# A Hymba-style layer on one core: mixer and experts joined into one program per engine, with a new order for the last tiles

## The reference

```python
h = concat([meta, x])                          # 4112 rows
hn = rms_norm(h, mix_norm_g)
q, k, v, B, C, H = split(hn @ w_in)            # 512 | 128 | 128 | 512 | 512 | 512 columns
a = sliding_window_sink_attention(rms_norm(q), rms_norm(k), v, sinks, rel_bias)  # 128-row blocks, own and previous keys
c = B * conv3_causal(C * H)
h = h + concat([rms_norm(a), rms_norm(c)]) @ w_out
hn = rms_norm(h, ffn_norm_g)
# router: the best of 4 groups, then the best 2 of its 8 experts, gate = p(group) * softmax(top 2)
# tokens sorted by expert; each expert works through its tokens in blocks of 128 rows
h = h + gate * ((silu(x @ w_gate[e]) * (x @ w_up[e])) @ w_down[e])
return h[16:]
```

## Time and profile before

| | us |
|---|---|
| median of 3 runs | 2775.46 (2773.0 to 2777.52) |
| profiled execution | 2770.24 |
| its span in the trace | 2768.6 |
| TensorE busy in the span | 2646.2 (96%) |
| VectorE busy | 1721.2 (62%) |
| ScalarE busy | 1394.0 (50%) |
| GpSimd busy | 832.8 (30%) |
| transfers, all queues | 495.22 MB, mean 179 GB/s |

### The profile page before, as it was taken

The page is one execution under the profiler, slowest core; times in us unless marked ns, Lnnn a source line. Parts: engine busy times, 40 slices in busy tenths (PEclk is TensorE's granted clock), DMA queues, the critical chain, the costliest instruction groups (busy, mean ns, idle before and its releaser), DMA issues.

```text
span 2768.6 us, 49889 instructions
## 1 busy us (share of the span) xinstructions
PE 2646.2 (96%) x14252; PEld 1820.5 (66%) x14253; DVE 1721.2 (62%) x3920; ACT 1394.0 (50%) x3046; POOL 832.8 (30%) x825
## 2 busy tenths in 40 slices
PE   4999999999999999996599999999999999999997
PEld 2445555555555555553488888888888888888886
DVE  5677777777777777776445456545545444546643
ACT  7665555556555556653234455445545443445533
POOL 1133333233333323331223333223323322333332
PEclk9899999999999999998799999999999999999999
DMA  8376666666666666656556677676767665667763
GB/s 310 85 164 165 155 159 159 151 156 163 165 154 158 159 152 156 165 133 153 183 159 189 197 223 241 191 223 200 240 189 235 204 187 155 180 188 232 241 182 53
DMA packets 546395, 495.22 MB, mean 179 GB/s; under 512 B 411787, under 2 KB 411948, under 8 KB 545340
## 3 DMA queue, kind: packets, MB, share of 16 engines
q1 hardware_dynamic: 517516, 406.08, 52.1%
q0 software_dynamic: 28848, 88.77, 13.7%
HBM read 309.74 MB, written 87.88 MB: 144 GB/s over the span
## 4 chain that ended last, share of the span: by engine, by line
PE 49%; DMA 1%; issue 0%; DVE 0%; POOL 0%; ACT 0%; POOLq 0%; DVEq 0%; ACTq 0%
PE psB L1637 15%; PE psA L1637 15%; PE psF L1637 8%; PE psG L1637 8%; PE psC L1645 1%; PE psD L1645 1%; PE psE L1652 1%; DMA xg<-hn_rows,slots 1%; DMA slots<-slot_table 0%; DMA out_rows<-y,rows_of_y 0%; DVE down_lo L1773 0%; DVE y L1780 0%; POOL out_rows L1573 0%; ACT gT_hi L1757 0%; POOL slots_old L1578 0%
## 5 line engine op out<-in xcount | busy, mean ns | idle before, releaser
L543 PE MATMUL psG<-wi_all,both_xT 128*128 128x512 f16 x1536 | 345.2, 381 | 11.2 <-DMA both_xT<-x 11.2
L543 PEld LDWEIGHTS psG<-wi_all,both_xT 128*128 128x128 f16 x1536 | 148.7, 98 | 188.4 <-DMA both_xT<-x 11.4
L1561 POOL DMA_INDIRECT xg<-hn_rows,slots x80 | 100.8, 1261 | 542.4 <-DMA slots<-slot_table 392.0
L1637 PE MATMUL psB<-up_hi,gT_hi 128*128 128x512 f32 x632 | 254.1, 402 | 0.0
L1637 PE MATMUL psA<-gate_hi,gT_hi 128*128 128x512 f32 x632 | 246.8, 391 | 3.1 <-ACT gT_hi L1757 1.7
L1773 DVE TENSOR_TENSOR down_lo<-wi_all,down_hi 128x512 fp32r<-128x512 f32 x256 | 157.0, 685 | 147.3 <-ACT down_hi L1731 147.3
L1637 PE MATMUL psB<-up_hi,gT_lo 128*128 128x512 f32 x632 | 247.4, 391 | 0.0
L1637 PE MATMUL psA<-gate_hi,gT_lo 128*128 128x512 f32 x632 | 246.9, 391 | 0.0
L1637 PE MATMUL psA<-gate_lo,gT_hi 128*128 128x512 f32 x632 | 246.6, 390 | 0.0
L1637 PE MATMUL psB<-up_lo,gT_hi 128*128 128x512 f32 x632 | 246.3, 390 | 0.0
L1757 ACT ACTIVATE gT_hi<-psC 128x512 fp32r<-128x512 f32 x80 | 47.8, 598 | 384.2 <-PE psC L1645 384.2
(11 more groups left out here) (315 smaller groups left out, 5902.9 us busy)
## 6 DMA issues: line engine op xcount, KB each, us to landing
wi_all<-in_w_gate SPq DMA_DIRECT2D x32, 2048.0 KB, 9.8
wi_all<-in_w_up SPq DMA_DIRECT2D x32, 2048.0 KB, 12.8
wi_all<-in_w_down SPq DMA_DIRECT2D x32, 2048.0 KB, 12.0
xt<-in_x SPq DMA_DIRECT2D x32, 512.0 KB, 3.8
um<-u_rows SPq DMA_DIRECT2D x64, 256.0 KB, 2.8
out_rows<-h SPq DMA_DIRECT2D x32, 512.0 KB, 3.2
xres<-in_x SPq DMA_DIRECT2D x31, 512.0 KB, 4.7
hn_rows<-xres SPq DMA_DIRECT2D x31, 512.0 KB, 2.9
```

Of the source, the lines that this page charges most:

```text
L543: m = nc.tensor.matmul(ps, left[:, l, k, :], weights.half(r, k, n, width), start=(k == opens and j == 0), stop=(k == closes and j == 2))
L1561: pool.indirect_dma_start(xg[:], None, hn_dram, bass.IndirectOffsetOnAxis(ap=slots[:, 0, 0:1], axis=0), bounds_check=SEQ + P - 1).then_inc ...
L1637: m = nc.tensor.matmul(ps[:, :], l[:, k, :], r[:, r_k[n], :], start=(n == 0 and j == 0), stop=(n == len(l_k) - 1 and j == 2))
```

## The change

- `mixer` and `experts` no longer open a block. Each returns one function per engine, and one block runs, on each engine, the mixer's and then the experts' function.
- In place of the barrier, each engine calls `mixed`: six waits on constants, for the last counts, the last router exponentials, the 18 last steps, the last scatter into the lists, and the last stores of output rows and of `hn`. ScalarE's table load and VectorE's clearing of `slots` come before `mixed`, its clearing of `y` after it.
- For that, the semaphores of both stages live to the end, and `slots`, `slots_old`, `rows_of_y` are allocated ahead of the mixer's tiles.
- The last tile's list entries have tiles of their own (`slot_last`, `entry_last`), so that its `place_tokens` doesn't wait for the scatter of the tile before.
- On GpSimd, in every tile, the convolution's first product is put ahead of the wait for `um`, and two semaphore increments are added.
- In the written-out end: on SP `store_u(32)` goes ahead of `turn_a(31)`, `load_shifted(32)` ahead of `load_residual(31)`; on TensorE `values(32)` ahead of `counts_of(30)`, and `out_half(32)` is completed before `route(31)`; on VectorE `place_tokens(29)` goes ahead of `lower_prob(31)`, `attended(32)` ahead of `lower_c(32)`, and `place_tokens(30)` behind `lower_hn(31)`.

```diff
         with ExitStack() as ctx:
-            mixer(nc, ctx, locals())
+            mix, mixed = mixer(nc, ctx, locals())
         with ExitStack() as ctx:
-            experts(nc, ctx, locals())
+            serve = experts(nc, ctx, locals())
+        with nc.Block() as block:
...
+            @block.gpsimd
+            def _(pool):
+                mix["gpsimd"](pool)
+                serve["gpsimd"](pool)
...
+    slot_last, entry_last = sb("slot_last", [P, 2], I32), sb("entry_last", [P, 2, 2], I32)
+
+    def lists(t):
+
+        return (slot_last, entry_last) if isinstance(t, int) and t == TILES else (slot, entry)
...
         turn_hn(t - 2)
+        store_u(t)
         turn_a(t - 1)
-        store_u(t)
+        load_shifted(t)
         load_residual(t - 1)
-        load_shifted(t)
...
         out_half(t - 1, aT_in, FIRST_CHUNKS)
+        values(t)
         counts_of(t - 2, t)
-        values(t)
         out_half(t, cT_in, LAST_CHUNKS)
+        out_half(t, aT_in, FIRST_CHUNKS)
         route(t - 1, t)
-        out_half(t, aT_in, FIRST_CHUNKS)
...
-                after(pool, um_in, t)
                 after(pool, u_s, t)
                 after(pool, c_hi, t - 1)
                 after(pool, c_lo, t - 1)
+                hold(pool, held)
                 g.tensor_tensor(yc[:], u[:], w_cv[:, 2, :], ALU.mult).then_inc(cv.sem, 1)
+                after(pool, um_in, t)
+                hold(pool, held)
                 g.tensor_tensor(um[:, 0, :], um[:, 0, :], w_cv[:, 1, :], ALU.mult).then_inc(cv.sem, 1)
...
-            after(dve, listed, t - 1)
+            where, what = lists(t)
+            gates = what[:].bitcast(F32)
+            if what is entry:
+                after(dve, listed, t - 1)
...
         top_scores(t - 1)
+        place_tokens(t - 3)
         lower_prob(t - 1)
-        place_tokens(t - 3)
...
         choose_experts(t - 2)
+        add_residual(t - 1)
+        attended(t, t - 3)
         lower_c(t)
-        add_residual(t - 1)
-        place_tokens(t - 2)
-        attended(t, t - 3)
         scale_hn(t - 1)
         lower_a(t)
         lower_hn(t - 1)
+        place_tokens(t - 2)
...
+    def mixed(eng):
+
+        eng.wait_ge(cnt_ps.sem, cnt_ps.at(TILES))
+        eng.wait_ge(rt_e.sem, rt_e.at(TILES))
+        eng.wait_ge(last, planned)
+        eng.wait_ge(listed.sem, listed.at(TILES))
+        eng.wait_ge(rows_out.sem, rows_out.at(TILES))
+        eng.wait_ge(hn_out.sem, hn_out.at(TILES))
...
         s.preload_act_table_set("silu_and_others")
+        mixed(act)
...
         v.tensor_copy(slots[:, :, 0], cst[:, C_JUNK:C_JUNK + 1].to_broadcast([P, 4])).then_inc(cleared, 1)
+        mixed(dve)
         v.memset(y[:], 0.0).then_inc(cleared, 1)
```

82 lines of the change are left out of this document (47 added, 35 removed).

## The result

| | before | after |
|---|---|---|
| median | 2774.23 (4 runs, 2769.07 to 2777.52) | 2750.97 (4 runs, 2750.46 to 2751.34) |
| profiled execution | 2770.24 | 2750.93 |
| its span | 2768.6 | 2749.3 |

A forecast was written before the change was run, and what follows sets the result against it. TensorE alone was taken to bound both steady parts, so only the hole between stages could pay: -8.4 to the last list landing and -6.1 at the seam, -14.5 in all, from 2775.46 to 2761.0 us, range 2754 to 2769.5.

The forecast's parts named there:

- The seam: Between mixer and experts: drain and barrier go, saving 6.6 us, less 0.5 for a disturbed gather: -6.1, bounds -6.9 and -4.6.
- the second rival: At the barrier: GpSimd's 6.03 us drain is work someone must await, so the gain there is 0.6; 2767.0, chance 0.10.
- The concern: First gather: SP's next 2 MB load starts earlier, into the gather, costing nothing to 2 us; 0.5 taken.
- project_kv(32): Last tiles: its 2.62 us wait for `place_tokens(29)` goes, so `out_half(31)` ends 2.6 us earlier.
- values(32) to out_half(32): End of mixer: `out_half(32)` starts about 1279.5 and runs its second half at once, before `route(31)`: 7.4 us gained by its end.
- The last list entry and its landing: Tile 32's list scatter: issued 10.3 us earlier, landing about 1320.0 beside the expert load: -8.4, bounds -10.3 and -5.5.
- lower bound of 17.2: Whole kernel: the largest gain from the known bounds, -17.2 against the forecast -14.5, giving a median of 2758.3.
- An edit can only pay, or cost, in the hole: Whole kernel: only about 1273 to 1349 us can change, since TensorE alone sets the time in both stages' steady parts.
- The step to the median: From profile to median: the profiled execution lies 5.2 below the runs' median, so 2755.7 becomes 2761.0.
- The first (the order gives little): End of mixer: `out_half(32)` stays as late as before, leaving only the list wait and barrier gains, -7.1; 2768.4, chance 0.13.
- The third (slower through GpSimd beside VectorE): Steady tiles: GpSimd's earlier product slows VectorE beyond its slack of 1.9 us a tile; 2790 at 2.9 lost, chance 0.05.
- The fourth (more than forecast): Hole: full clock in `out_half(32)`, scatter landing in 2.1, undisturbed gather, earlier start: -19.1, 2756.4, chance 0.10.

The follow-up runs named there:

- no_tokens29: The changed kernel with `place_tokens(29)` behind `lower_prob(31)` again on VectorE: 2755.38 us, 0.9939 of before.
- pe_route_first: The changed kernel with `route(31)` between the two halves of `out_half(32)` again on TensorE: 2751.51 us, 0.9925 of before.
- no_sp: The changed kernel with SP's order of the last tiles as before: 2754.2 us, 0.9938 of before.
- order_gather_safe: The changed kernel with VectorE's old order for tile 32, block counts read later, first `down` loaded after the first gather, second `gate` after the second: 2748.98 us.
- router_early2: The changed kernel with block counts read later, expert loads held behind gathers, and tile 31's router steps earlier: 2747.88 us, 2748.36 us when repeated.
- conv_only: The kernel before with only GpSimd's first convolution product ahead of the wait for `um`: 2769.74 us, 0.9985 of before.
- no_conv: The changed kernel with GpSimd's first convolution product behind the wait for `um` again: 2751.1 us, 0.9924 of before.
- tail_only: The kernel before with only the new written-out orders of the last tiles on SP, TensorE and VectorE: 2762.78 us, 0.9964 of before.
- seam_only: The kernel before with only the joined program, six waits for the barrier and three small tiles allocated earlier: 2768.96 us, 0.9989 of before.
- seam_gather_alone: The kernel before with only the joined program, plus an SP wait holding the second expert's `gate` until the first gather lands: 2766.83 us, 0.9978 of before.
- no_attended_first: The changed kernel with VectorE's order of before for tile 32: 2755.55 us, 0.9947 of before.
- no_dve_pe: The changed kernel with VectorE's order of before for tile 32 and TensorE's end order of before: 2761.67 us, 0.9964 of before.

## Why the prediction was right and wrong

**The seam** (-6.1 forecast). The read of the blocks came 0.35 us after the landing, 0.3 forecast; the drain was a fixed cost of 6.03 us, as assumed, so the second rival falls. The gather was not disturbed and was even faster, 4.7 us instead of 5.3, where I had added 0.5. From landing to product 13.46 us, 14.75 forecast: 1.3 better, nearly all of it from the gather. The concern was right in kind and badly bounded: "nothing to 2 us" for a load that starts into a gather should have been "nothing to 5". That the changed kernel escaped it was luck: it turned on whether the load began 0.1 or 0.7 us before the end of the gather's issue.

**project_kv(32)** (-2.6). The stretch before it is 2.8 shorter. Right, and no_tokens29 gives 2.07 for it with all else changed.

**values(32) to out_half(32).** I gave the start 8.15 us after out_half(31), and it was 7.26: `lower_c(32)` was done 4.7 us after it, as forecast, and the way from there took 2.5 instead of 3.5; the row with the slow first bank (5.04 against 4.44) cost 0.6 of that again. The end came 20.07 after out_half(31), 20.8 forecast. The mechanism for TensorE's order holds: 5.7 us with VectorE's order of before. What the prediction didn't see is that VectorE's new order alone brings 3.7 of it and then costs 1.4. `place_tokens(30)` behind `lower_hn(31)`, taken as costing nothing and given no gain, has 2.2 of the 3.0 us by which `hn` is ready sooner. So the wait of 4.12 us, which the prediction gave to TensorE's order, would have all but gone without it: 0.32 us of it are left in pe_route_first.

**The last list entry and its landing.** From the end of out_half(32) to the second scatter 23.93 us, 23.9 forecast. The landing took 3.98, the 4.0 taken from between the bounds. The Trainium skill's page "DMA: Bandwidth & Descriptors", section "Queues, rings and completion order", has the DMA engines take turns between queues; by that the prediction had a landing near 2.1. The trace lies between: the scatter of tile 32, issued beside the load's last microseconds, took 4.0 us, one of tile 31, well inside it, 6.2. The latter was issued at 1303.91 and the load flowed until about 1315, so it did not stand behind all of it, in which the trace agrees with the page. Of the 2.45 to 2.9 us of wait that the list tile takes away, 0.6 arrive, 1.0 forecast.

**The terms that were missed.** Against the forecast span of 2754.1 the trace has 2749.3, 4.8 less: 2.6 up to `project_kv(32)`, 0.3 to out_half(31), 0.7 in out_half(32), 1.3 in the seam, less 0.15 behind it. The span moved by 19.3, more than the prediction's own lower bound of 17.2. The step that failed is "An edit can only pay, or cost, in the hole": the start was put at nothing, and 2.5 of the 2.6 us lie ahead of the third tile. The windows view there, in before:

```profile
170.00:180.00 10.00, 7.23 (x37) 3.71 (x36) 8.16 (x34) 3.32 (x12) 3.17 (x3) 0.83 0.76 189
```

The same in after:

```profile
170.00:180.00 10.00, 7.71 (x45) 4.11 (x44) 8.46 (x38) 4.26 (x13) 4.39 (x4) 1.00 0.77 211
```

The granted clock was 0.83 and 1.00; 1.3 of the 2.5 us lie behind the wait for VectorE in this stretch, 0.5 in it (2.76 and 2.27 us) and the rest ahead of it. A second such place is from 60 to 120 us, where the clock was 0.86 in both, but 0.77 in no_tokens29, no_sp and order_gather_safe among others. router_early2 shows both cases with one program, so a part of it differs from execution to execution; but all four runs of no_tokens29 took some 2 us more than its wait explains, while seven of the changed kernel's eight lie within 0.9 us, so a part seems to hang on the kernel. Whether it is the joining, or GpSimd's product, which does act in the first tiles, is open: conv_only is 2.9 faster in the median, but no_conv, with the product back behind its wait, is as fast as after.

**The step to the median.** The other 5.2 us were a mistake of method, the step "it lies 5.2 below the median of the runs, so the median becomes". The profiled execution was 5.2 below the median of three, and I carried that distance over as if it belonged to the profiler. In 62 further runs the kernel before took 2767.87 to 2779.31 us with a median of 2772.2, and the time follows the mean granted clock: 2776.0 on average at 0.981 (4 runs), 2772.7 at 0.983 (28), 2768.7 at 0.985 (3). So of the 5.2 the profiled execution was 2.0 on the quick side, and the median of the first three runs 3.2 on the slow side. The changed kernel's four runs in the table have 0.985 to 0.987 and lie within 0.9 us, so its profile equals its median. A forecast made from span to span would have given 2755.7.

**The rivals.** The first (the order gives little) falls: out_half(32) ends 5.5 us earlier after out_half(31). The third (slower through GpSimd beside VectorE) falls: TensorE's 300 us of 300, VectorE's 231.82 against 232.29. Its pair of rows was also read too simply: the 1.25 us step had a GpSimd product beside it as well, one that began 0.25 us behind it and took 2.13 us, where the same product of tile 32, which began ahead of VectorE's step beside it, took 1.26. So in this pair the operation that began second was the one that paid, on either engine. The fourth (more than forecast) names some of what came, the gather and the earlier start of out_half(32), but not the clock through its first bank and not the landing. It gave 2756.4, still 5.4 too high, for the same false step to the median.

**The parts don't add up to the whole.** In medians beside their own runs of before: tail_only -9.9, seam_only -3.7, conv_only -2.9, and the list tile's 1.2 make 17.7, where the whole has 21.2 in that comparison (2750.93 against 2772.08). A part of the missing 3.5 is what seam_only lost by its gather: with seam_gather_alone's -5.3 in its place the sum is 19.3. The rest may lie in the start, since the third tile begins 2.5 to 5.5 us later in the profiles of these parts than in after's, but that isn't shown.

**Open.** Why the gather's issue takes 1.87 us in some kernels and 1.1 to 1.5 in others; it repeats within a kernel, as the medians of no_attended_first and no_dve_pe show, so it isn't pure chance. Why the start is quicker in after than in before (2.5 us). Whether router_early2 with `lower_c(32)` first would be better still was not tried.

## What to carry to other kernels

A barrier between two stages can be paid for mostly by one engine's fixed drain: look for it in the sequencer's rows, and join the programs if the stages can meet at semaphores. Before you take credit for removing a wait, look which other edit of the same change already removes it, and which transfer the earlier work will now meet: a gather beside a large load cost 4 to 5 us of the 7 that the barrier's end gave. And forecast from span to span; the distance of one profiled execution to the median of three runs is mostly spread, not an offset.

## What the runs showed of the hardware that I had not expected

- GpSimd's drain at the end of a block: 6.029 us in all five kernels with the barrier, whatever went before. ScalarE's on the same line took 0.23 us, VectorE's 0.02.
- An indirect gather of 128 rows whose issue overlaps the start of a 2 MB load landed after 4.6 to 5.1 us (seven profiles) when 0.1 us of its issue were still to come as the load began, and after 9.7 to 9.9 (three profiles) when 0.7 us were. Two later gathers with 0.8 us still to come took 9.1 and 9.9. With no load beside it an issue of 1.88 us landed in 5.2.
- A shift of the tiles by 96 bytes a partition changes the transfers' busy share from 0.66 to 0.59 at the same bytes per second, and the time by nothing that shows: this column alone says little of how close the transfers are to a limit.
- TensorE's granted clock around a wait of 2 to 3 us early in the kernel fell in one profiled execution (0.78 from 170 to 180 us) and stayed at 1.00 in another of the same program. From the end of the wait to the third tile it cost 2.9 us.
